# A conditional's joined norm, written into both branches instead of behind them

## The reference

```python
x = x + moe_ffn(h, router_w, w1, w3, w2)         # first block, layer 1
x = rmsnorm(x, final_norm_g)                     # first block's last norm
# second block, layer 0
shift_m, scale_m, gate_m, shift_f, scale_f, gate_f = split(silu(c) @ ada_w[0] + ada_b[0], 6)
h = rms_norm(x, g_pre_mix[0]) * (1.0 + scale_m) + shift_m
q, k, v, u = split(h @ w_in[0] + b_in[0])        # then attention and pooling
```

## Time and profile before

| | us |
|---|---|
| median of 3 runs | 2087.17 (2086.82 to 2090.17) |
| profiled execution | 2089.91 |
| its span, first to last instruction | 2088.1 |
| busy: PE, DVE, ACT, POOL | 2020.0, 1627.6, 1187.9, 72.8 |
| the join (last sum of the experts to the first query product) | about 1523 to 1544 |

### The profile page before, as it was taken

One profiled execution on the slowest core, in us unless ns is written; L12 is line 12 of the kernel. 1 busy time (PEld: TensorE's weight loads), 2 busy tenths in 40 slices (PEclk: granted clock), 3 DMA queues, 4 the chain that ended last, 5 costly groups with the idle time before them and its releaser, 6 DMA issues.

```text
span 2088.1 us, 24564 instructions
## 1 busy us (share of the span) xinstructions
PE 2020.0 (97%) x10120; PEld 1675.5 (80%) x10120; DVE 1627.6 (78%) x1556; ACT 1187.9 (57%) x1264; POOL 72.8 (3%) x97
## 2 busy tenths in 40 slices
PE   7999999999999999999999999999979999899998
PEld 6888788878887778888888888888767787787887
DVE  5777889756878779888988888888976986676454
ACT  6444454446454367777777777777735444444443
POOL 0000010000000000000000000001010000100000
PEclk9999999999999989999999999999989999999999
DMA  8443479854444458999999999999953898434551
GB/s 307 156 162 139 144 282 386 333 212 179 162 143 155 150 229 331 378 367 379 360 376 370 355 378 377 386 374 385 397 206 132 339 372 302 184 137 173 190 182 61
DMA packets 80321, 554.77 MB, mean 266 GB/s; under 512 B 9286, under 2 KB 11206, under 8 KB 14534
## 3 DMA queue, kind: packets, MB, share of 16 engines
q1 hardware_dynamic: 74160, 536.45, 67.9%
q10 hardware_dynamic: 5468, 14.60, 1.9%
q0 software_dynamic: 576, 2.10, 0.3%
HBM read 548.30 MB, written 4.82 MB: 265 GB/s over the span
## 4 chain that ended last, share of the span: by engine, by line
PE 86%; DVE 8%; ACT 3%; POOL 1%; issue 1%; DMA 1%; ACTq 0%; POOLq 0%; DVEq 0%
PE bank L455 81%; PE bank L482 2%; DVE wlo L1135 2%; ACT whi L1128 1%; POOL small L2363 1%; DVE xn L1715 1%; DMA raw<-in_moe_up 1%; DVE scoresB L1727 1%; DVE gate_tanh L1711 0%; DMA cols<-in_cols 0%; DVE x L2112 0%; DVE xn L2122 0%; PE bank L575 0%; PE bank L960 0%; DVE hTlo L1639 0%
## 5 line engine op out<-in xcount | busy, mean ns | idle before, releaser
L1135 DVE TENSOR_TENSOR wlo<-raw,whi 128x2048 fp32r<-128x2048 f32 x459 | 1045.5, 2285 | 268.1 <-ACT whi L1128 265.2
L1128 ACT ACTIVATE whi<-raw 128x2048 fp32r<-128x2048 f32 x459 | 876.2, 1913 | 355.5 <-PE bank L455 286.5
L455 PE MATMUL bank<-whi,hThi 128*128 128x512 f32 (+1 forms) x1088 | 430.0, 395 | 17.0 <-DVE hTlo L1639 7.4
L455 PE MATMUL bank<-whi,hTlo 128*128 128x512 f32 (+1 forms) x1088 | 421.7, 388 | 0.0
L455 PE MATMUL bank<-wlo,hThi 128*128 128x512 f32 (+1 forms) x1088 | 421.7, 388 | 0.0
L455 PE MATMUL bank<-whi,slots_hi 128*128 128x512 f32 x704 | 275.1, 391 | 2.4 <-DVE wlo L1135 2.3
L455 PE MATMUL bank<-whi,slots_lo 128*128 128x512 f32 x704 | 274.3, 390 | 0.0
L455 PE MATMUL bank<-wlo,slots_hi 128*128 128x512 f32 x704 | 274.2, 389 | 0.0
L455 PEld LDWEIGHTS bank<-whi,hThi 128*128 128x128 f32 x1088 | 208.0, 191 | 69.6 <-issue 14.0
L455 PEld LDWEIGHTS bank<-whi,hTlo 128*128 128x128 f32 x1088 | 208.1, 191 | 41.7
L455 PEld LDWEIGHTS bank<-wlo,hThi 128*128 128x128 f32 x1088 | 208.2, 191 | 39.5 <-issue 1.0
(11 more groups left out here) (332 smaller groups left out, 2269.8 us busy)
## 6 DMA issues: line engine op xcount, KB each, us to landing
raw<-in_moe_up SPq DMA_DIRECT2D x176, 1024.0 KB, 7.1
raw<-in_moe_down SPq DMA_DIRECT2D x88, 1024.0 KB, 7.0
raw<-in_w_in SPq DMA_DIRECT2D x72, 1024.0 KB, 4.8
raw<-in_ada_w SPq DMA_DIRECT2D x48, 1024.0 KB, 6.9
raw<-in_second_up SPq DMA_DIRECT2D x44, 1024.0 KB, 4.9
raw<-in_ffn_up SPq DMA_DIRECT2D x22, 1024.0 KB, 5.3
raw<-in_second_down SPq DMA_DIRECT2D x22, 1024.0 KB, 5.0
raw<-in_w_out SPq DMA_DIRECT2D x16, 1024.0 KB, 5.2
```

Of the source, the lines that this page charges most:

```text
L455: m = mm(dst, l_, r_, start=start and i == 0, stop=stop and i == len(pairs) - 1)
L1128: s.then_inc(s.unit.activation(split_slots(p)[0][:, 0:n], slot_of_ring(raw, p, NRAW)[:, 0:n], ACT.Copy), ("hi", p), sem="weights_hi")
L1135: e.then_inc(e.unit.tensor_tensor(lo[:, 0:n], slot_of_ring(raw, p, NRAW)[:, 0:n], hi[:, 0:n].bitcast(F32), ALU.subtract), ("lo", p), sem=sem)
```

## The change

`two_ways` gets a fourth argument. Where ScalarE and VectorE give it, it is run inside each of the two ways, at the end, behind `ways_joined`; the code that both ways join begins later. ScalarE's joined part becomes a function `joined()`, which gets one new line: the high part of the first query piece is made behind the DMAs of the attention's tables. VectorE's `joined()` gets the low part of it ahead of the second tile's low parts, and `normed(0)` stays behind the join. TensorE's and POOL's programs are not changed, and SP's list is the same.

```diff
-        def two_ways(e, sparse, dense):
+        def two_ways(e, sparse, dense, behind=None):
...
                 e.own()
                 board.part = ""
                 e.unit.sem_inc(board.sem(e.done + "_way_end"), 1)
+                if behind is not None:
+                    e.passed, e.last = dict(start["passed"]), None
+                    ways_joined(e)
+                    behind()
                 return e.pieces, [e.counts.get(z) for z in ("weights_hi", "weights_lo")]
...
-            e.passed, e.last = dict(start["passed"]), None
+            if behind is None:
+                e.passed, e.last = dict(start["passed"]), None
+                ways_joined(e)
             if isinstance(e, Tensor):
                 e.held = {}
-            ways_joined(e)
...
+            def joined():
+                square_sum(x3[:, 1], 1, 1, ("squares", "final", 1))
+                features((0, "mix2"), None, (0,))
+                s.wait_ge(("gained", 1))
+                s.own()
+                square_sum(xn3[:, 1], 1, 3, ("squares", "modulated", 0, 0, 1))
+                load_attention(0)
+                s.split_ahead(("q2", 0, 0), 1)
+                features((0, "mix2"), None, (1,))
+
...
-                    two_ways(s, lambda: sparse_experts(l), lambda: dense_experts(l))
-            square_sum(x3[:, 1], 1, 1, ("squares", "final", 1))
-            features((0, "mix2"), None, (0,))
-            s.wait_ge(("gained", 1))
-            s.own()
-            square_sum(xn3[:, 1], 1, 3, ("squares", "modulated", 0, 0, 1))
-            load_attention(0)
-            features((0, "mix2"), None, (1,))
+                    two_ways(s, lambda: sparse_experts(l), lambda: dense_experts(l), joined)
             load_gate(0, 0)
...
+                v.split_ahead(("q2", 0, 0), 1)
                 features((0, "mix2"), None, (1,))
-                normed(0)
...
-                    two_ways(v, lambda: sparse_experts(l), lambda: dense_experts(l))
-            joined()
+                    two_ways(v, lambda: sparse_experts(l), lambda: dense_experts(l), joined)
+            normed(0)
```

## The result

The changed kernel is slower: 2091.98 us (2083.35 to 2097.26, 21 runs) against 2086.82 us (2082.96 to 2091.08, 21 runs) in the same session, a ratio of 1.0021 with a 95% interval of 1.0013 to 1.0028. The forecast was 2084.9, with a range of 2082.4 to 2088.4. The profiled execution of the changed kernel took 2093.4 us, with a span of 2091.6.

The account below looks back on a forecast made before the run. The prediction took TensorE's products to bound the kernel nearly everywhere, so only its waits could shorten. 2.95 + 1.60 - 2.25 = 2.3 us of gain led to a forecast median of 2084.9 us, range 2082.4 to 2088.4.

Parts of the forecast that it names:

- The join: At the experts' end, `probT` follows VectorE's sums without a jump, so `xn` and TensorE start earlier: gain 2.95 us.
- The first query piece: Its high and low parts fill idle time of ScalarE and VectorE, so TensorE's first query product needn't wait: gain 1.60 us.
- the sum: Over the whole kernel, 2.95 + 1.60 - 2.25 gives a gain of 2.3 us.
- The jump is still taken: At the key transposes, TensorE waits because ScalarE and VectorE jump later: a new wait of 2.25 us.
- the surcharge: At the new jump, extra cost from busy DMA queues: between 0 and 2.8 us, taken as 0.5.
- Nothing here can lose except the surcharge: Bound on the whole change: only the jump's extra cost among DMA loads, 0 to 2.8 us, could lose time.
- The fetch is late: slower: At the new jump, surcharge at its upper bound; TensorE waits 4.55 us, then low clock: 2091.3 us, chance 0.08.
- The clock falls at the new wait: Behind the key transposes' wait, products run at a low clock: gain 0.65, time 2086.5 us, chance 0.22.
- The jump is hidden: At the new jump, under 0.8 us beside last instructions, so no new wait: gain 4.55, 2082.6 us, chance 0.12.
- The stall isn't the jump's: At the join, 2.6 us belong to the joined code's first instructions; only 1.60 is gained: 2085.6 us, chance 0.08.

Follow-up runs that it names:

- J: The changed kernel with padding, later row loads and SP's 1 MB held, plus VectorE's first join product waiting for POOL's second root instruction; ratio 0.9994 to the kernel before.
- A: The changed kernel plus eight never-run idle instructions that shift VectorE's code behind the join; ratio 0.9998 to the kernel before.
- C: The changed kernel with the three loads of modulation rows moved behind the first tile's softmax; ratio 1.0009 to the kernel before.
- H: The kernel before plus 31 never-run idle instructions, putting VectorE's jump target near a code block's end; ratio 1.0004 to the kernel before.
- E: The changed kernel plus eight never-run idle instructions and SP's next 1 MB held until the second tile's keys are done; ratio 0.9995 to the kernel before.
- F: The changed kernel plus eight never-run idle instructions and the loads of modulation rows issued later; ratio 0.9996 to the kernel before.
- I: The changed kernel with its two ways in the other order, so the jump comes at the experts' entry; ratio 1.0018 to the kernel before.
- D: The changed kernel with eight never-run idle instructions, later loads of modulation rows and SP's next 1 MB held; ratio 0.9986, again 0.9985, to the kernel before.
- G: The kernel before, without the moved join, with modulation rows loaded later and SP's next 1 MB held; ratio 1.0001 to the kernel before.

## Why the prediction was wrong, step by step

**The join, 2.95: right in kind, 2.13 in size.** `probT` starts 0.31 after the sums, not 0.11, and `xn` does not find POOL's root done. POOL's timeline after the change:

```profile
1521.80 0.19 POOL L2402 TENSOR_SCALAR small<-small 128x1 f32<-128x1 f32 x1 [74.62 <-DVEq L1171]
1522.09 1.13 POOL L2405 TENSOR_SCALAR small<-small 128x1 f32<-128x1 f32 x1
1523.30 0.57 POOL L2407 TENSOR_TENSOR small<-small,cst 128x1 f32<-128x1 f32 x1
```

The second instruction took 1.13, until VectorE's `probT` (1521.86 to 1523.09) was done; in J, ahead of `probT`, it takes 0.26. I had taken POOL's times from a trace in which VectorE stood in its jump meanwhile. The Trainium skill ("SBUF — State Buffer", SBUF: two separate sides) says that GpSimd and a VectorE instruction with two inputs from SBUF take one shared port in turn, for a whole instruction each; `probT` has two such inputs, and the rows agree.

**The first query piece, 1.60: right.** The first query product follows without a gap. TensorE was through with its 24 products at 1548.03 - 6.99 = 1541.04, that is 22.00 after the experts' last product, where the prediction has 1542.85 - 1520.97 = 21.88. That the two agree so well is luck: the clock was back at 1.00 after 13.49 us, where it took 16.84 before, and this made up for the join's missing 0.8. (The prediction's 1547.39 for the key transposes before is the chain's row; the timeline has 1547.23, which changes nothing in the sum.)

**The jump is still taken, a wait of 2.25: this step failed.** The wait was 6.99. That the jump would be bare on VectorE, that `utok` would be the releaser and that ScalarE would jump first is as the profile after has it; the surcharge was mis-sized, and a part of it wasn't in the sum. The path was another one too: the sum has VectorE wait for ScalarE's high part, but ScalarE's branch ended at 1534.02, ahead of SP's 1 MB, its next instruction came 2.43 later (2.56 in the kernel before), without any surcharge, and the high part was done at 1539.71. VectorE, whose branch came 0.70 later, bore it all and had `utok` at 1545.11. I took 0.5 as "near the lower end" of 0 to 2.8 since "the nearest row is the quiet jump itself". VectorE's jump in the kernel before costs 2.97 from branch to next instruction, the new one 5.27: 2.3 more, near the upper end. The working had itself said that SP issues 1 MB at that moment, and the table above shows that this is what holds the packet. And the target's place in its block, which the prediction doesn't ask for, added 3.06 (A, C and H). Together 5.4 instead of 0.5. "Nothing here can lose except the surcharge" failed with it.

**The rivals.** "The fetch is late: slower" had 0.08 and happened in kind: its surcharge of 2.8 was nearly met at 2.3, and its low clock came (windows above). That its time of 2091.3 is only 0.7 below the median is luck: it has a wait of 4.55 and no second stall, where the wait was 6.99, and 4.1 for two batches at the low clock, where 2.27 was lost. The rival's argument against itself, "a jump's code is little and has a queue of its own", was the error: the queue is its own, but its packet came 3.41 after the branch, with 1 MB just ahead, and 0.96 with that held. That the two share the DMA engines is the likely reason; no run shows it apart. "The clock falls at the new wait" happened within it, at a price of 2.27; that the length of the wait decides, as it argues, is not borne out by A, C, E and F. "The jump is hidden" did not happen. "The stall isn't the jump's" is refuted by I.

**The sum.** 2.13 of the join plus 1.60 would have stood against a wait of 0.9 to 1.5, as D has it: 2.2 to 2.8. D's gain of 0.15%, 3 us, is the size of the forecast's 2.3; against G's trace it is 1.3 to 2.0. As far as these intervals can tell, the mechanism of the forecast holds where the fetch is quiet.

## What to carry to other kernels

A jump that is moved takes its stall with it, so price it by what the DMA queues carry at the new place, not by what it cost at the old one; and look at whether its target stands near the end of a block, since a few instructions that are never run can move it. Where several causes share one wait (here SP's transfer, the block's end, the rows' loads), one or two repairs gave 0.23 to 0.26% against the changed kernel (A, E, F; C's 0.12% is within the noise), all together 0.35%. And when an engine's duration is taken over from the trace, ask what its neighbours did meanwhile.

## What the runs showed of the hardware

- A code packet of 8 KB started up to 2.4 us later where one 1 MB transfer had been issued 0.13 to 0.33 us ahead of the end of the branch (after, A, F against D, E, J).
- Eight instructions that are never run, put ahead of a jump's target, took 3.06 us of stall away (A), and 31 of them made one of 1.03 (H).
- A jump at the experts' entry: TensorE stood 7.41 us (I) where it stands 1.29 without it. Why it is dearer there than 3 us isn't settled; the DMA engines were busy for 0.83 of the time from 751.8 to 755.0, and no kernel took that away.
- The granted clock fell to 0.50 behind waits of TensorE of 1.84 and 2.45 us (E, C) and stayed at 1.00 behind 2.43 and 2.69 (F, A).
- A small GpSimd instruction takes 0.26 us beside an idle VectorE and 1.13 beside a VectorE product of two SBUF inputs of 1.23.
